# A hybrid decoder layer with 32 experts: residual kept on chip, overflow tables earlier, and a bias spread by DMA

## What is computed

```
x = x + mix @ w_out[l]
h = rms_norm(x, ffn_norm_g[l])
logits = h @ router_w + router_b                       # 32 experts
top_val, top_idx = lax.top_k(logits, 4)
gates = softmax(top_val)
# for each block of token slots of one expert e
hid = h[tok] @ w1[e] + b1[e]                           # w1[e]: 1024 x 2048
glu = min(hid[..., ::2], 7); lin = clip(hid[..., 1::2], -7, 7)
out = (glu * sigmoid(1.702 * glu) * (lin + 1)) @ w2[e] + b2[e]   # w2[e]: 1024 x 1024
x = x + sum over a token's experts of out * gate
return rms_norm(x, final_norm_g)
```

## Time and profile before

| | us |
|---|---|
| median of 3 runs | 1572.97 |
| lowest and highest | 1569.95, 1578.02 |
| the profiled execution | 1575.28 |
| its span in the trace | 1573.5 |
| PE, DVE, ACT, POOL busy | 97%, 48%, 34%, 23% |
| mean granted clock of TensorE | 0.982 |
| HBM read, written | 442.89 MB, 22.71 MB |

### The profile page before, as it was taken

One profiled execution on the slowest core, in us unless ns is written; L12 is line 12 of the kernel. 1 busy time (PEld: TensorE's weight loads), 2 busy tenths in 40 slices (PEclk: granted clock), 3 DMA queues, 4 the chain that ended last, 5 costly groups with the idle time before them and its releaser, 6 DMA issues.

```text
span 1573.5 us, 28685 instructions
## 1 busy us (share of the span) xinstructions
PE 1519.7 (97%) x11426; PEld 877.3 (56%) x11426; DVE 749.2 (48%) x818; ACT 542.5 (34%) x626; POOL 360.8 (23%) x432
## 2 busy tenths in 40 slices
PE   9999999999998899999999999999999999999994
PEld 7777878775553455444455444455444455444453
DVE  5599756442434534334444334443334443334443
ACT  5434333311223333324333334333334333333333
POOL 5643642413121001111111211121212111212100
PEclk9999999999999999999999999999999999999997
DMA  6322011110559999999999999999999999999993
GB/s 192 112 80 80 13 17 56 55 55 30 227 225 350 362 351 385 384 391 388 387 392 396 384 386 391 383 396 388 384 385 390 385 396 386 390 383 391 400 379 123
DMA packets 97356, 458.28 MB, mean 291 GB/s; under 512 B 23041, under 2 KB 37031, under 8 KB 48142
## 3 DMA queue, kind: packets, MB, share of 16 engines
q1 hardware_dynamic: 87486, 436.58, 70.9%
q0 software_dynamic: 9664, 20.31, 5.7%
q10 hardware_dynamic: 144, 0.52, 0.1%
HBM read 442.89 MB, written 22.71 MB: 296 GB/s over the span
## 4 chain that ended last, share of the span: by engine, by line
PE 83%; DVE 10%; DMA 3%; issue 2%; ACT 2%; SPq 0%; DVEq 0%; POOLq 0%; POOL 0%; ACTq 0%
PE banks L1801 41%; PE banks L1787 8%; PE banks L1789 7%; PE banks L1788 7%; PE banks L1726 2%; PE banks L1818 1%; PE banks L1782 1%; DMA x_sum<-xs 1%; DMA slots<-in_expert_w_dram 1%; PE banks L1514 1%; PE banks L1399 1%; PE banks L1794 1%; PE banks L1400 1%; PE banks L1401 1%; PE banks L1579 1%
## 5 line engine op out<-in xcount | busy, mean ns | idle before, releaser
L1801 PE MATMUL banks<-slots,BK 128*32 128x512 f32 x6144 | 667.3, 593 | 0.0
L2143 DVE TENSOR_TENSOR lo<-slots,hi 128x2048 fp32r<-128x2048 f32 x128 | 293.1, 2293 | 395.1 <-ACT hi L1175 335.3
L1801 PEld LDWEIGHTS banks<-slots,BK 128*32 128x32 f32 x6144 | 195.8, 110 | 449.3 <-issue 448.6
L1175 ACT CAST hi<-slots 128x2048 fp32r<-128x2048 f32 x128 | 243.2, 1903 | 314.5 <-DMA slots<-in_expert_w_dram 308.9
L1787 PE MATMUL banks<-lo,a_hi 128*128 128x512 f32 x496 | 201.1, 406 | 7.5 <-DVEq L2387 4.4
L964 POOL DMA_INDIRECT x_sum<-hT,idy x32 | 47.1, 1473 | 658.5 <-issue 583.2
L1789 PE MATMUL banks<-hi,a_lo 128*128 128x512 f32 x496 | 195.4, 394 | 0.0
L1788 PE MATMUL banks<-hi,a_hi 128*128 128x512 f32 x496 | 194.7, 393 | 0.0
L1787 PEld LDWEIGHTS banks<-lo,a_hi 128*128 128x128 f32 x496 | 93.8, 189 | 51.3 <-issue 23.3
L2332 DVE TENSOR_TENSOR a_lo<-banks,a_hi 128x768 fp32r<-128x768 f32 x31 | 29.7, 958 | 189.8 <-ACT a_hi L1264 189.8
L1789 PEld LDWEIGHTS banks<-hi,a_lo 128*128 128x128 f32 x496 | 93.9, 189 | 20.6
(11 more groups left out here) (401 smaller groups left out, 1620.9 us busy)
## 6 DMA issues: line engine op xcount, KB each, us to landing
slots<-in_expert_w_dram SPq DMA_DIRECT2D x384, 1024.0 KB, 8.4
slots<-in_w_in_dram SPq DMA_DIRECT2D x13, 1024.0 KB, 5.2
xs<-in_x_dram SPq DMA_DIRECT2D x8, 512.0 KB, 4.8
slots<-in_w_out_dram SPq DMA_DIRECT2D x2, 2048.0 KB, 8.9
x_sum<-xs SPq DMA_DIRECT2D x4, 512.0 KB, 17.3
h_rows<-slots SPq DMA_DIRECT2D x4, 512.0 KB, 2.6
xs<-x_sum SPq DMA_DIRECT2D x4, 512.0 KB, 4.8
x_sum<-xs POOLq DMA_DIRECT2D x3, 512.0 KB, 11.1
```

The lines of the kernel that those rows point to most:

```text
L1175: nc.scalar.copy(w2_hi[j][:, :, :], raw[n % RAW]).then_inc(hi_ready, 1)
L1801: ins = nc.tensor.matmul(bank[2 + g][j * CB:(j + 1) * CB, :], xT[q][:, k, g * CB:(g + 1) * CB], raw[n % RAW][:, j, :], start=(k == 0), sto ...
L2143: tensor_tensor(raw_lo[n % RAW][:, :, :], raw[n % RAW], w2_hi[j][:, :, :], ALU.subtract).then_inc(lo_ready, 1)
```

## The change

1. **The residual stays in `xs`.** SP's four stores of it and POOL's four accumulating DMAs are gone. `x_sum` is instead filled with zeros by POOL at the start, all 640 rows in one DMA (before: only the 128 spare rows). The b2 results are added to `xs` by DVE straight from PSUM, four adds of 128 x 1024, ahead of `overflow_blocks` in block 1; ACT's four copies are gone. `b2r` moves to `lnw` and `lnb`, so its cast waits for b2's own loads alone. At the end SP reads `x_sum` into `slots`, and DVE adds each tile to `xs` before ACT squares it.
2. **Overflow tables first.** In block 2, `overflow_rows` stands behind w1 unit 2 instead of unit 5, and `overflow_tables` ahead of the four low parts instead of behind them.
3. **The bias b1 by DMA.** `biasrows`, `b1r`, `sel`, `set_expert`, `biases` and `keep_bias` are gone. SP issues for each expert one DMA (`load_bias`, L615) that reads the four quarters of b1[e] 32 times each and writes 128 partitions of 512 columns (256 KB) into one of two buffers `bias_rows`. The first two are issued among the small loads ahead of the expert weights, the other 30 in `next_units` ahead of the load of unit 4. In `swiglu` DVE waits for the DMA, adds 1.0 on the odd columns, and then adds the bias to the bank as before.

The diff, cut to its core:

```diff
+        def load_bias(eng, e, q):
+            eng.dma_start(bias_rows[q],
+                          b1[0, bass.ds(e, 1), :].rearrange("a (j f) -> (a j) f", j=4).unsqueeze(1).to_broadcast([4, CB, CW]))\
+               .then_inc(bias_loaded[q], 16)
...
             sp.dma_start(g2row, ffn_norm_g.to_broadcast([P, D])).then_inc(g2_in, 16)
-            for j in range(4):
-                sp.dma_start(biasrows[j * E:(j + 1) * E, :], b1[0, :, j * CW:(j + 1) * CW]).then_inc(bias_in, 16)
...
+            for q in range(2):
+                load_bias(sp, q, q)
...
-                sp.dma_start(x_sum[tt * P:(tt + 1) * P, :], xs[:, tt, :]).then_inc(sums_started[tt], 16)
...
-            def next_units(i, q, e, e_before):
+            def next_units(i, q, e, e_before, bias=True):
                 for u in range(UNITS):
                     n = q * UNITS + u
                     wait_used(sp, i, n - RAW)
+                    if bias and u == 4:
+                        load_bias(sp, e, q)
                     if u < W1U:
                         load_w1(sp, e, u, n)
                     else:
                         load_w2(sp, e_before, u - W1U, n)
...
-                sp.dma_start(xs[:, tt, :], x_sum[tt * P:(tt + 1) * P, :]).then_inc(sum_in[tt], 16)
+                sp.dma_start(sum_back[tt], x_sum[tt * P:(tt + 1) * P, :]).then_inc(sum_in[tt], 16)
...
-            for q, rows in enumerate((h2_rows, x_sum)):
-                pool.dma_start(rows[T:T + SPARE, :], zrow).then_inc(store_done[q], 16)
+            pool.dma_start(h2_rows[T:T + SPARE, :], zrow).then_inc(store_done[0], 16)
+            pool.dma_start(x_sum.rearrange("(n p) d -> p n d", p=P), zrow.unsqueeze(1).to_broadcast([P, TT + 1, D]))\
+                .then_inc(store_done[1], 16)
...
-            for tt in range(TT):
-                pool.wait_ge(sums_started[tt], 16)
-                pool.wait_ge(b2_taken, tt + 1)
-                pool.dma_start(x_sum[tt * P:(tt + 1) * P, :], b2_rows[tt], accum_op=ALU.add).then_inc(b2_in, 16)
...
                     if st == ("o", 2, 1):
-                        act.wait_ge(sums_started[0], 16)
-                        act.wait_ge(hrow_ready, TT + 1)
+                        act.wait_ge(b2_in, 16 * 6)
                         for half in range(2):
-                            filled(act, "h2T", 0, half)
-                        for half in range(2):
-                            nc.scalar.copy(b2r[:, half * CW:(half + 1) * CW], b2_half[half]).then_inc(b2_split, 1)
-                    if st == ("o", 2, 0):
-                        act.wait_ge(bias_raised, 1)
-                        nc.scalar.copy(b1r[:, 0, :], biasrows).then_inc(bias_split, 1)
+                            nc.scalar.copy(b2r[half][:, :], b2_half[half]).then_inc(b2_split, 1)
...
-            def biases(b, q):
-                pe.wait_ge(sel_set, b + 1)
-                for part in range(2):
-                    nc.tensor.matmul(bank[bias_bank][:, :], sel[:, q, :], b1r[:, part, :], start=(part == 0), stop=(part == 1))
...
-            def swiglu(i, b, n, first=False):
-
+            def swiglu(i, b, n, q, first=False):
+
+                dve.wait_ge(bias_loaded[q], i * 16 + 16)
+                tensor_scalar(bias_rows[q][:, 1:CW:2], bias_rows[q][:, 1:CW:2], 1.0, None, ALU.add).then_inc(bias_raised, 1)
                 wait_used(dve, i, n)
-                dve.wait_ge(bias_kept, b + 1)
-                tensor_tensor(inner, hid, bias_row.unsqueeze(1).to_broadcast([P, NG, CW]), ALU.add).then_inc(hid_free, 1)
+                dve.wait_ge(bias_raised, b + 1)
+                tensor_tensor(inner, hid, bias_rows[q].unsqueeze(1).to_broadcast([P, NG, CW]), ALU.add).then_inc(hid_free, 1)
...
-                set_expert(q, e)
                 act_low(b - 1)
+                if overflow:
+                    overflow_tables()
                 for j in range(W2U):
                     low_part(i, W2U * (q - 1) + j, q * UNITS + W1U + j, j)
-                if overflow:
-                    overflow_tables()
...
             act_low(0)
+            for tt in range(TT):
+                dve.wait_ge(b2_full, tt + 1)
+                rows = xs[:, tt, :].rearrange("p (h f) -> p h f", h=2)
+                tensor_tensor(rows, rows, b2_banks, ALU.add).then_inc(b2_taken, 1)
             overflow_blocks()
...
             for tt in range(TT + 1):
+                if tt < TT:
+                    dve.wait_ge(sum_in[tt], 16)
+                    tensor_tensor(xs[:, tt, :], xs[:, tt, :], sum_back[tt], ALU.add).then_inc(sum_added, 1)
```

More of the change, by code:

```diff
@@ L183, in hymba_layer @@
         inner = gated(region(qk[:, :, :, :].rearrange("p a j t -> p (a j t)"), 0, NG * CW))
-        bias_row = region(qk[:, :, :, :].rearrange("p a j t -> p (a j t)"), NG * CW, CW)
+        bias_rows = [region(qk[:, :, :, :].rearrange("p a j t -> p (a j t)"), NG * CW + n * CW, CW) for n in range(2)]
         BW = JT * NC * 2 * C
@@ L204, in hymba_layer @@
         gatesT = rounded("gatesT", "BK", BW, 2 * CW, [3 * E, T])
-        b2r = rounded("b2r", "xs", TT * D, 0, [3 * E, D])
-        b2_rows = [xs[:, 1, :], xs[:, 2, :], xs[:, 3, :], region(hTf, 2048, D)]
+        sum_back = [region(slot_flat[0], n * D, D) for n in range(TT)]
         slot0, slot1 = (region(sbf, n * TT * NS, TT * NS).rearrange("p (t s) -> p t s", t=TT) for n in range(2))
@@ L231, in hymba_layer @@
         lnb = sb("lnb", [P, HW])
+        b2r = [rounded(f"b2r_{nm}", nm, HW, 0, [3 * E, CW]) for nm in ("lnw", "lnb")]
         rw = sb("rw", [P, KT, E])
         rb = sb("rb", [P, E])
-        expert_row = sb("expert_row", [P, E])
-        row_block = sb("row_block", [P, 4])
         fb = sb("fb", [H, 1])
@@ L332, in hymba_layer @@
         g1_spread = sem("g1_spread")
-        bias_in = sem("bias_in")
+        b2_in = sem("b2_in")
+        bias_loaded = [sem(f"bias_loaded{q}") for q in range(2)]
         small_in = sem("small_in")
@@ L392, in hymba_layer @@
         idy_copied = sem("idy_copied")
-        sums_started = [sem(f"sums_started{t}") for t in range(TT)]
         gates_set = sem("gates_set")
@@ L732, in next_units @@
                         load_w2(sp, e_before, u - W1U, n)
-            next_units(0, 1, 1, 0)
+            next_units(0, 1, 1, 0, bias=False)
             with sp.Fori(1, E // 2) as i:
@@ L952, in gather, with add_rows @@
                     .then_inc(xg_loaded[q], 16)
-            def add_rows(i, q, b, first=False):
-                if first and q == 0:
-                    pool.wait_ge(b2_in, 16 * TT)
-                    pool.wait_ge(store_done[0], 16)
+            def add_rows(i, q, b):
                 nc.gpsimd.tensor_copy(idy[:, q:q + 1], idx_all[:, bass.ds(b, 1), 0]).then_inc(idy_copied, 1)
@@ L970, in _ @@
             gather(3, 1)
[L971 to L975 removed]
+            add_rows(1, 0, 0)
             gather(4, 0)
@@ L1271, in scale_rows @@
                               slot_gates[:, bass.ds(b, 1)]).then_inc(y_scaled, 1)
-            def keep_bias(i, b, n, first=False):
-                wait_used(act, i, n)
-                if not first:
-                    act.wait_ge(hid_free, b)
-                nc.scalar.copy(bias_row, bank[bias_bank][:, :]).then_inc(bias_kept, 1)
             def sigmoid(b):
@@ L1301, in _ @@
             act.sem_inc(y_scaled, 1)
-            def take_b2(tt):
-                act.wait_ge(b2_full, tt + 1)
-                if tt < TT - 1:
-                    act.wait_ge(sums_started[tt + 1], 16)
-                    act.wait_ge(rows_scaled, 1)
-                nc.scalar.copy(b2_rows[tt].rearrange("p (h f) -> p h f", h=2), b2_banks).then_inc(b2_taken, 1)
             act.wait_ge(gT_full, 1)
@@ L1312, in _ @@
             act_high(0)
-            for tt in range(TT):
-                take_b2(tt)
-            keep_bias(0, 1, UNITS)
             filled(act, "o", TT - 1, 1)
@@ L1775, in b2_product @@
                     ins = nc.tensor.matmul(bank[6 + half][:, :], gatesT[:, tt * P:(tt + 1) * P],
-                                           b2r[:, half * CW:(half + 1) * CW], start=True, stop=True)
+                                           b2r[half][:, :], start=True, stop=True)
                 ins.then_inc(b2_full, 1)
@@ L1842, in block_work @@
                     w1_unit(i, q * UNITS + k, k, q)
-                    if k == 5 and overflow:
-                        pe.wait_ge(bias_kept, b + 1)
+                    if k == 2 and overflow:
                         overflow_rows()
@@ L2184, in _ @@
             dve.wait_ge(consts_ready, 4)
-            step(nc.vector.tensor_reduce(expert_row[:, :], ident[:, :].rearrange("p (j e) -> p e j", j=4), AX, ALU.add))
-            step(nc.vector.tensor_reduce(row_block[:, :], ident[:, :].rearrange("p (j e) -> p j e", j=4), AX, ALU.add))
             tensor_tensor(rw[:, :, :], rw[:, :, :], vec("g2").unsqueeze(2).to_broadcast([P, KT, E]), ALU.mult).then_inc(rw_ready, 1)
@@ L2291, in _ @@
                         for half in range(2):
```

(2 more changed lines are left out.)

66 lines of the change are left out of this document (16 added, 50 removed).

## The result

| | us |
|---|---|
| changed kernel, median of 4 runs | 1696.05 (1692.43 to 1700.32) |
| kernel before, 4 runs beside it | 1574.36 (1569.95 to 1578.02) |
| ratio, 95% interval | 1.0776, 1.0752 to 1.0800 |
| forecast | 1618, range 1575 to 1640 |
| span, mean granted clock | 1695.0, 0.968 |

Slower, as forecast, but by 122 us and not by 45: outside the range. Rival D (above 1640) has the size. The other, dearer small pieces, is a part of the cause, though not because the engines are four.

The account below looks back on a forecast made before the run. PE sets the pace with the DMA engines nearly full; the bias load makes DMA the bound. +61 - 5 - 0.9 - 7.5 + 1.2 + 3.6 - 7.0 = +45.4 on 1575.28 gives 1620.7, 1618 on the median; range 1575 to 1640.

Parts of the forecast that it names:

- Rival D: Bias load: repeated reads collide or small pieces are already slower; 3.7 us or more per block, above 1640; chance 0.05.
- The bound and the split: Expert loop: PE sets the pace; the bias load runs on 4 engines and makes the DMA engines the bound.
- The price of the load: Expert loop: bias load adds 2.7 us per block, 35.8 instead of 33.77; +61 us over 30 loads.
- The base: Expert loop: a block's DMA without the bias load takes 33.1 us, between 31.3 and 33.77.
- The 5 us absorbed once: Expert loop: activations are ready 5.2 us before PE takes them, absorbing part of the delay once; -5 us.
- The tables ahead: Block 2, near 545 us: PE's 4.44 us idle and the half-clock stretch behind it go; -7.0 us.
- The wait at 425 us: Before block 0: ACT's b2 cast no longer waits for the residual's store, removing PE idle and half clock; -7.5 us.
- Block 1: overflow_blocks now runs after DVE's b2 adds, so low parts start later and PE waits longer; +1.2 us.
- The end: Kernel's tail: DVE adds ahead of ACT's squares, three of four on the path; +3.6 us, bounds +1.2 and +4.9.
- The zero fill: Start: POOL's x_sum fill grows from 128 to 640 rows; taken as 0, bounds 0 and +3 us.
- B: Bias load spreads over 16 engines: 1562, or 1548 if the DMA engines have room; chance 0.13.
- C: Bias load on four engines, but DMA base only 31.3 to 32 us per block: 1562 to 1585; chance 0.05.

Follow-up runs that it names:

- Run 4: Changed kernel, but one bias load of 128 different w2 rows to 128 partitions, on 16 engines; 1582.82 us, ratio 1.0057.
- Run 1: Changed kernel without the 30 bias loads in the expert loop (b1 wrong in the output); 1558.99 us, ratio 0.9902.
- run 3: Changed kernel, but four bias loads per expert of 32 partitions each, on 16 engines, each address read 32 times; 1642.19 us, ratio 1.0437.
- run 5: Changed kernel, but four bias loads per expert of 32 different w2 rows to 32 partitions each, on 16 engines; 1640.97 us, ratio 1.0417.
- run 10: Changed kernel, but two bias loads per expert of 64 different w2 rows to 64 partitions each, on 16 engines; 1642.10 us, ratio 1.0424.
- run 2: Changed kernel, bias load still on four engines, but reading 128 different w2 rows, no address twice; 1697.55 us, ratio 1.0788.
- run 6: Changed kernel, but one bias load reading one 2 KB address 128 times into 128 partitions, on 16 engines; 1584.65 us, ratio 1.0054.
- run 9: Changed kernel, but four bias loads per expert, each to all 128 partitions in 512-byte pieces of different rows, on 16 engines; 1588.68 us, ratio 1.0085.
- run 7: Changed kernel with the bias by matmuls as in the kernel before, so residual on chip and tables first remain; 1567.35 us, ratio 0.9953.
- run 8: Kernel before with only the overflow tables moved first; 1566.42 us, ratio 0.9948.
- run 11: Kernel before with tables first and b2r in lnw and lnb, cast early; residual still through x_sum; 1563.32 us, ratio 0.9919.

## Why the prediction was wrong

**The bound and the split: right.** PE set the pace with nothing to spare in the DMA engines, the bias load runs on four engines (4 completions per load), it makes the DMA the bound, and PE idles in each block for a unit that has not landed. PE idles 3.8 us a block, though, and not 2 (89.5 us of 900, 23.6 blocks), the share fell to 0.97 and not to 0.94, and 351 GB/s flow and not 374.

**The price of the load: wrong, and this is the step that failed.** "A block then takes 33.1 + 2.7 = 35.8 us"; it took 38.15. Three sizes were off in the same direction.

- The base. I took 33.1 us for the DMA engines' own block. Run 4 puts it higher: 34.17 less 8 pieces of 86 ns is 33.5. Run 1 puts it at 33.42 or less. +0.3 to +0.4.
- The piece. I priced a 2 KB piece at 78 to 90 ns, by its bytes at the mean rate. It measured 120: 32 x 0.120 = 3.84 us, and not 2.7. Run 4 shows 86 ns for the same piece in a load of 128 partitions, and runs 3, 5 and 10 show 114 or 115 on 16 engines, so the rule (bytes by rate) was good for the wide form alone. +1.1.
- The others. I let the twelve other engines go on at their pace and only wait. But the weights' pieces beside the load rose to 427 ns (315 beside the load of run 4); three quarters of them took over 350 ns, in run 4 0.2%. 38.15 - 33.5 - 3.84 leaves about 0.8 us a block for it.

Measured as differences between runs, the load's 38.15 - 33.42 = 4.73 us a block are 0.75 for its bytes spread well (run 4), 2.1 more in loads of 32 or 64 partitions (runs 5 and 10 against 4), and 1.9 more on four engines instead of 16 (run 2 against 5). The forecast had only the first and the third in mind. The third holds something else that I can't take apart: PE's granted clock is at half for 51 of the 900 us in the changed kernel and for 65 in run 2 (where I looked, at 684, 988 and 1066 us, around a wait of PE of some 4.5 us), and never in runs 3 to 6, 9 and 10. As run 2, with more of it, has the same block, it hardly weighs much.

The bound failed with it: 36.7 as the upper end came from two rates of wide loads, and no row of the kernel before had a narrow load beside a full stream. The range should have been open there: its end of 1640 was set by a period of 36.5, and the period was 38.15. With the measured 3.84 us on the old upper base, 33.77 + 3.84 = 37.6 a block, the same sum gives 1673; the slowed weights are the rest.

**The 5 us absorbed once: too small.** Blocks 2, 3 and 4 ran at 33.6, 35.9 and 37.4 us, so the lead of the weights absorbed some 7.5 us before the full period was reached.

**The tables ahead: right**, -7.6 in the changed kernel from block 2's W1 to block 3's, bias matmuls included, -7.2 in runs 7 and 8, against -7.0. Nothing was late behind them.

**The wait at 425 us: right as far as single traces tell**, -8.2 at block 0's W1 against -7.5 and half of the 0.9 for the first two pairs of matmuls; in runs 7 and 11, where the matmuls stay, -6.5 and -6.3. **Block 1**: +1.2 forecast; PE's wait for the low part grew by 0.9, and the way from block 0's W1 to block 2's by 2.1 in the changed kernel and by 0.9 in run 7. **The end**: +3.6 forecast, +3.7 measured (25.5 from PE's end instead of 21.8). **The zero fill**: 0 was taken, and block 0 starts earlier, so no cost shows; runs 7 and 11, with and without it, start block 0 at 446.5 and 446.7.

**The rivals.** B decided by the packet count, which went against it; but its time (1562 with no cost for the load) would not have come true with 16 engines in quarters either: 1642. C, more room in the DMA engines, has nothing for it: even run 4's eight pieces an engine make the block 0.75 us longer. Of D, runs 2, 5 and 6 exclude the repeated address. Its other half, that small pieces may be slower, gave "3.7 us or more", and 3.84 were measured; but the pieces are about as slow on 16 engines (115 ns), so it isn't the four engines that make them dear. D had a chance of 0.05.

## What to carry to other kernels

A small load beside a full stream is not priced by its bytes: look at how it is split. One load with 128 partitions outermost cost 0.75 us a block for 256 KB, the same bytes in loads of 32 or 64 partitions 2.8 to 2.9, and on four engines 4.7, in good part because the stream's own pieces slow down too. And even the cheapest of these loses here to the two small matmuls: a block is 34.17 us with it and 33.77 with them. And of a change with several parts, the gain may sit in a detail: the earlier cast was worth 3 us here (run 11 against 8), while keeping the residual on chip cost 4 (run 7 against 11), most of it at the end.

## What the runs showed of the hardware

- 32 or 128 reads of the same 2 KB took as long as reads of different rows (120 and 120 ns on four engines, 85 and 86 on 16).
- A load of 64 partitions disturbs a stream into all 128 as much as one of 32: the stream's 8 KB pieces take 379 and 382 ns instead of 315.
- The DMA share doesn't show this. Over all bias loads of the loop it was 1.01 at 339 GB/s in run 5 and 1.02 at 417 in run 4: a busy engine can be one that is held up.
